# A mixture-of-experts block on one core: the last expert's down weights loaded early, and the sums at the end rearranged

## The reference, cut to what matters

```python
h = rmsnorm(x, norm_ffn_w)
logits = h @ w_router + b_router
top_logits, top_idx = lax.top_k(logits, 4)              # 4 of 32 experts
top_w = softmax(top_logits)
# for each expert e, over the tokens that chose it:
gu = xb @ w_gate_up[e] + b_gate_up[e]                   # 1024 -> 2048
gate = min(gu[:, ::2], 7.0); up = clip(gu[:, 1::2], -7.0, 7.0)
act = (up + 1.0) * (gate * sigmoid(gate * 1.702))
ys = act @ w_down[e] + b_down[e]                        # 1024 -> 1024
# y[token] = sum over its 4 choices of top_w * ys
out = rmsnorm(x + y, norm_final_w)
```

## Time and profile before

| | us |
|---|---|
| median of 3 runs | 1920.76 |
| lowest, highest | 1917.67, 1920.85 |
| the profiled execution | 1917.87 |
| its span, first to last instruction | 1916.1 |
| TensorE busy | 1861.3 |
| VectorE busy | 643.6 |
| ScalarE busy | 283.4 |
| GpSimd busy | 253.6 |
| mean granted TensorE clock | 0.99 of 2.4 GHz |

### The profile page before, as it was taken

The page is one execution under the profiler, slowest core; times in us unless marked ns, Lnnn a source line. Parts: engine busy times, 40 slices in busy tenths (PEclk is TensorE's granted clock), DMA queues, the critical chain, the costliest instruction groups (busy, mean ns, idle before and its releaser), DMA issues.

```text
span 1916.1 us, 40809 instructions
## 1 busy us (share of the span) xinstructions
PE 1861.3 (97%) x17222; PEld 870.7 (45%) x17222; DVE 643.6 (34%) x1225; ACT 283.4 (15%) x563; POOL 253.6 (13%) x297
## 2 busy tenths in 40 slices
PE   7999999999999999998999999999999999999995
PEld 4455555555555444442343444434343444444343
DVE  2563553635632110145132222323131322223236
ACT  3233423323233000021000000000000000000002
POOL 0010010000100000013222212121212222121200
PEclk9999999999999999998999999999999999999997
DMA  9211110111102321427999999999999999999995
GB/s 384 81 67 50 44 41 34 45 51 45 45 23 83 121 88 66 168 87 279 396 419 418 419 418 418 418 418 420 417 420 418 420 418 419 418 419 419 418 399 214
DMA packets 82218, 495.46 MB, mean 259 GB/s; under 512 B 15188, under 2 KB 15868, under 8 KB 28256
## 3 DMA queue, kind: packets, MB, share of 16 engines
q1 hardware_dynamic: 72656, 478.49, 61.7%
q0 software_dynamic: 9488, 15.94, 2.2%
HBM read 478.00 MB, written 24.53 MB: 262 GB/s over the span
## 4 chain that ended last, share of the span: by engine, by line
PE 50%; DMA 1%; DVE 1%; DVEq 0%; issue 0%; SPq 0%; ACT 0%; ACTq 0%
PE ps L1076 33%; PE ps L1091 17%; DMA arena<-expert_rows 1%; DVE oaT L1507 0%; DMA arena<-h_rows,gix 0%; DVE oaT L1504 0%; DVEq L2198 0%; DVE arena L1507 0%; DVEq L2149 0%; SPq L528 0%; DVEq L2141 0%; ACT arena L1495 0%; DVE arena L1504 0%; DVEq L2091 0%; DVEq L2103 0%
## 5 line engine op out<-in xcount | busy, mean ns | idle before, releaser
L1076 PE MATMUL ps<-arena 128*32 128x512 f32 x5952 | 647.4, 594 | 3.7 <-DVE arena L1504 3.7
L1076 PEld LDWEIGHTS ps<-arena 128*32 128x32 f32 x5952 | 202.6, 110 | 430.0 <-issue 425.2
L587 PE MATMUL ps<-hT,arena 128*128 128x512 f32 x768 | 349.4, 596 | 1.2 <-DVE arena L1507 0.9
L1091 PE MATMUL ps<-arena,hT 128*32 128x256 f32 x6144 | 339.0, 380 | 9.5 <-DMA arena<-in_w_dn 9.5
L1091 PEld LDWEIGHTS ps<-arena,hT 128*32 128x32 f32 x6144 | 209.0, 110 | 146.8 <-issue 29.5
L1504 DVE TENSOR_TENSOR arena<-ps,arena 128x768 f32<-128x768 f32 x64 | 58.3, 953 | 581.9 <-PE ps L1076 581.8
L587 PEld LDWEIGHTS ps<-hT,arena 128*128 128x128 f32 x768 | 138.4, 190 | 143.8 <-issue 139.6
L2259 POOL DMA_INDIRECT expert_rows<-hT,six x90 | 90.4, 1004 | 682.1 <-ACT hT L1158 663.7
L1451 ACT ACTIVATE arena<-arena 128x768 f32<-128x768 f32 x32 | 27.0, 844 | 696.5 <-DVE arena L2104 696.5
L587 PE MATMUL ps<-arena 128*128 128x512 f32 x256 | 120.2, 611 | 4.4 <-DVE arena L1504 2.2
L2247 POOL DMA_INDIRECT arena<-h_rows,gix x93 | 95.3, 1025 | 48.9 <-POOL gix L2244 27.2
(11 more groups left out here) (251 smaller groups left out, 1232.6 us busy)
## 6 DMA issues: line engine op xcount, KB each, us to landing
arena<-in_w_gu SPq DMA_DIRECT2D x256, 1024.0 KB, 16.4
arena<-in_w_dn SPq DMA_DIRECT2D x128, 1024.0 KB
arena<-in_w_pair SPq DMA_DIRECT2D x16, 1024.0 KB, 4.8
arena<-in_w_merge SPq DMA_DIRECT2D x16, 1024.0 KB, 4.8
expert_rows<-oaT SPq DMA_DIRECT2D x4, 2048.0 KB, 25.5
arena<-expert_rows SPq DMA_DIRECT2D x16, 512.0 KB, 15.1
arena<-in_x SPq DMA_DIRECT2D x8, 512.0 KB, 6.2
arena<-in_w_qb SPq DMA_DIRECT2D x4, 768.0 KB, 5.0
```

The lines of the kernel that those rows point to most:

```text
L587: ins = pe.matmul(region(name)[:, cols], lhsT, rhs, start=(k == 0), stop=(k == n - 1))
L1076: ins = pe.matmul(gu[32 * j:32 * (j + 1), g, :], columns[:, g, k, :], ring[k][:, 512 * j:512 * (j + 1)], start=(k == 0), stop=(k == KD - 1))
L1091: ins = pe.matmul(yd[32 * j:32 * (j + 1), g, 0:256], aT[:, g, 2 * c + k, :], ring[8 + c][:, D * k + 256 * j:D * k + 256 * (j + 1)], start= ...
```

## The change

The four down chunks of expert 31 no longer go through `ring[8..11]` at the end. They are loaded right after expert 0's own down chunks and the last tile of h2, into places of their own: parts of `hT`, `obT` and `oaT` that nobody uses later. For that, `tab`, `taby`, `tok` move together in `obT`, `wmT` and `bias_now` move to the arena, the running sum stays in `x2` in place of `acc`, and the last norm's weights go to `spare`.

VectorE transposes the last activations into a place of their own (`last_aT`, in the masks), so it doesn't wait for `down(30)`; it builds the join tables right after, the first and the second each with its own signal; then slots 0 to 2, then slot 3 by tile. All four tiles are finished by VectorE, each tile's finish behind the parts of the next. SP loads slots 0 to 3 one after the other, and the last norm's weights behind them. TensorE does tile 0's biases and first join, then `down(31)`, then the second join. The rows of extra blocks go to a second table `late_dram`, which is cleared like the first one, during pair 0 of the mixer.

```diff
@@ SP @@
+                if i == 0:
+                    for t in range(NT):
+                        sp.dma_start(late_dram[t * P * TOPK:(t + 1) * P * TOPK, :].rearrange("(p k) d -> p k d", k=TOPK),
+                                     zero_rows.unsqueeze(1).broadcast_to([P, TOPK, D])).then_inc(y_clear, 16)
...
             keep_rows(NT - 1)
+            def last_down_weights(c):
+                sp.dma_start(last_down[c], w_dn_chunk(NE - 1, 8 + c)).then_inc(last_down_in, 16)
+            last_down_weights(0)
+            ready(sp, f"lg{NT - 1}")
+            last_down_weights(1)
+            ready(sp, "x0_0", "x0_1")
+            sp.wait_ge(h2_st, 16 * NT)
+            last_down_weights(2)
+            last_down_weights(3)
             sp.wait_ge(table_set, 16 * NT * TOPK)
...
-            sp.dma_start(nrow, norm_final.broadcast_to([P, D])).then_inc(row_in, 16)
             sp.wait_ge(xT_done, NE - 1)
             sp.dma_start(tokens, token_row.broadcast_to([P, SEQ])).then_inc(row_in, 16)
-            for k in range(2):
-                early_slot(k)
-            down_weights(NE - 1, NE - 1)
-            for k in range(2, TOPK):
-                early_slot(k)
+            for k in range(TOPK):
                 sp.wait_ge(gu_used, 8 * (NE - 1) + 2 * k + 2)
                 sp.wait_ge(scattered, 16 * QUADS * min(NE - TOPK + 1 + k, JOINED[0]))
                 for t in range(NT):
+                    sp.dma_start(yin[k][:, t, :], slot_rows(y_dram, k, t)).then_inc(slot_in[k] if k < TOPK - 1 else rows_in[t], 16)
+            sp.dma_start(last_nrow, norm_final.broadcast_to([P, D])).then_inc(last_nrow_in, 16)
...
             for t in range(NT):
-                if t < AWAY:
-                    sp.wait_ge(all_rows, t + 2)
-                else:
-                    sp.wait_ge(out_done, t + 1 - AWAY)
+                sp.wait_ge(out_done, t + 1)
@@ TensorE @@
-            down(NE - 1)
...
             join(0, ys, 0)
+            last_expert_down()
+            pe.wait_ge(wm_done, 3)
             pe.wait_ge(ys_done, NE)
             join(1, last_ys, 0)
@@ ScalarE @@
-                if t < AWAY:
-                    ac.drain()
-                    copy(yin[1][:, t, :], acc[:, t, :], scale=r4[:, 1, t:t + 1]).then_inc(xn_done, 1)
...
-                if t:
-                    last_root(t - 1)
-            last_root(NT - 1)
+                last_root(t)
@@ VectorE @@
             activations(NE - 1)
-            activation_columns(NE - 1)
+            dv.transpose(last_aT.rearrange("p g b m -> p (g b m)"), act.rearrange("p g f -> p (g f)")).then_inc(aT_done, 1)
...
             for t in range(NT):
                 dv.wait_ge(rows_in[t], 48)
                 add_rows(TOPK - 1, t)
                 dv.drain()
-                add_parts(acc, t).then_inc(sum_done, 1)
+                if t:
+                    root(t - 1)
+                add_parts(t).then_inc(sum_done, 1)
                 dv.sem_inc(bo_kept, 1)
                 if t:
-                    root(t - 1)
-            for t in range(AWAY, NT - 1):
-                finish(t)
+                    finish(t - 1)
             root(NT - 1)
             finish(NT - 1)
@@ GpSimd @@
-            for t in range(AWAY):
-                po.wait_ge(xn_done, 2 * NT + t + 1)
-                po.tensor_tensor(x2[:, t, :], yin[1][:, t, :], nrow, ALU.mult).then_inc(all_rows, 1)
```

More of the change, by code:

```diff
@@ L537, in _ @@
             with sp.If(extra > 0):
-                sp.wait_ge(early_sums, TOPK - 1)
-                for t in range(NT):
-                    sp.wait_ge(rows_in[t], 48)
+                sp.wait_ge(bo_kept, NT)
                 with sp.Fori(0, MAX_EXTRA) as j:
@@ L1080, in up, with down_products, down @@
                         beside[k]()
-            def down(n):
+            def down_products(columns, weights, c):
+                for k in range(2):
+                    for g in range(QUADS):
+                        for j in range(4):
+                            ins = pe.matmul(yd[32 * j:32 * (j + 1), g, 0:256], columns[:, g, 2 * c + k, :],
+                                            weights[:, D * k + 256 * j:D * k + 256 * (j + 1)],
+                                            start=(c == 0 and k == 0), stop=(c == 3 and k == 1))
+                ins.then_inc(dn_used, 1)
+            def down(n, loads_before=0):
                 if not first(n):
@@ L1086, in down, with last_expert_down @@
                 for c in range(4):
[L1087 to L1094, removed]
+                    pe.wait_ge(chunk_in[8 + c], 16 * n + 16 - 16 * loads_before)
+                    down_products(aT, ring[8 + c], c)
+            def last_expert_down():
+                pe.wait_ge(last_down_in, 64)
+                pe.wait_ge(ys_done, NE - 1)
+                pe.wait_ge(aT_done, NE)
+                for c in range(4):
+                    down_products(last_aT, last_down[c], c)
             def expert(n):
@@ L1149, in _ @@
                         up(j + NE)
-                        down(j + NE)
+                        down(j + NE, loads_before=1)
         @block.scalar
@@ L2175, in _ @@
                 dv.wait_ge(again_in, 16 * NT * TOPK)
-                for k in range(TOPK - 1):
+                for k in range(TOPK):
                     add_slot(k)
+                dv.drain()
+                dv.memset(yin[TOPK - 1], 0.0)
                 for t in range(2):
@@ L2230, in _ @@
             po.wait_ge(tok_ready, 1)
-            po.wait_ge(y_clear, 16 * NT)
+            po.wait_ge(y_clear, 32 * NT)
             po.wait_ge(h2_st, 16 * NT)
@@ L2249, in gather, with scatter @@
                                           bounds_check=SEQ * 4 - 1, oob_is_err=False).then_inc(gathered, 16)
-            def scatter(n, q, passed=0):
+            def scatter(n, q, passed=0, into=y_dram):
                 if not first(n):
@@ L2258, in scatter @@
                 for g in range(QUADS):
-                    po.indirect_dma_start(out=y_dram.rearrange("r (j d) -> (r j) d", j=4),
+                    po.indirect_dma_start(out=into.rearrange("r (j d) -> (r j) d", j=4),
                                           out_offset=bass.IndirectOffsetOnAxis(ap=six[:, g:g + 1], axis=0),
@@ L2286, in _ @@
                         gather(j + NE, q)
-                        scatter(j + NE, q, passed=len(JOINED))
+                        scatter(j + NE, q, passed=len(JOINED), into=late_dram)
                         wait_past(scattered, 16 * QUADS * j + 16 * QUADS * (NE + 1 - len(JOINED)))
             po.sem_inc(all_rows, 1)
-            po.wait_ge(row_in, 48)
-            for t in range(AWAY):
-                po.wait_ge(xn_done, 2 * NT + t + 1)
-                po.tensor_tensor(x2[:, t, :], yin[1][:, t, :], nrow, ALU.mult).then_inc(all_rows, 1)
 def constants():
```

59 lines of the change are left out of this document (32 added, 27 removed).

## The result

The changed kernel took 1909.02 us in the median of five runs (1906.42 to 1909.33), the kernel before 1917.94 (1917.04 to 1920.85): and the ratio on record for the two sets of runs is 0.9946, 95% interval 0.9933 to 0.9959 (the two medians alone would give 0.9953). That is 0.5% faster, where 1909.5 was forecast. The profiled execution took 1906.42 us with a span of 1904.5, the lowest of the five; against the profiled execution of before it is 11.6 us shorter in the span, while the medians are 8.9 us apart.

What follows compares the result with a forecast made beforehand. TensorE bounds the loop, only just; bytes bound the end, 4 MB of weights then 4 MB of expert rows. -12.6 + 2.5 + 0.5 = -9.6 us gives 1908.3 or 1911.2, middle 1909.5; 8-in-10 range 1904.5 to 1915.

Steps and rivals of the forecast that it cites:

- The front: Four early loads before the table's read: they end near 884 to 885, delaying it 0.5 us, bounds 0 to 2.4.
- The start of slot 3: VectorE at the end: slot 3's first tile starts at 1881.6 instead of 1894.18, 12.6 us earlier.
- an end that was priced too high: From slot 3's first tile to the last store: 24.4 us, where before it was 21.9.
- the first rival: Before the loop, the table's completion waits for loads in flight: 1911.5, or 1912 with TensorE's clock; chance 0.14.
- The tile's step: VectorE at the end, per tile: slot 3, root, parts and finish in one row, 5.3 us.
- the rearrangement: VectorE's new order at the end, with two finishes back on VectorE: costs 2.5 us.
- The lead of about 3 us: Expert loop's weight stream: beyond 3 us of lead, pushed-in loads make TensorE wait at the last experts; 1916.5; chance 0.04.
- Slow landing of slots 2 and 3: At the end, rows come late: 1917 if slot 2 lands at 1884, 1913 more likely; chance 0.12.
- The blocked table: Before the loop, early loads ending after 885.9 hold up the table's read and TensorE; up to 1924; chance 0.04.
- The zeros: 8 MB more of writes for late_dram in the mixer's pair 0: cost taken as 0.
- TensorE's path: At the end: second join done at 1882.4, VectorE wants the parts at 1883.1; 0.7 us behind the bound, not showing.
- the signs that I had named: Table read within 1 us of 885.9, hole before up(1) 3.7 to 4.5 us, VectorE not waiting for rows, steps 5.3.

Runs made afterwards that it cites:

- late weights: The changed kernel with expert 31's four down chunks issued at the end again, between slots 1 and 2; 1921.06 us.
- the weights behind the table: The changed kernel with all four early chunks issued behind the table's read, in front of expert 1's chunks; 1916.61 us.
- two and two: The changed kernel with two early chunks loaded in the idle stretch, the other two behind the table's read; 1911.9 us.
- the quarter experiment: The changed kernel with only the last of the four early chunks loaded behind the table's read; 1908.24 us.
- the version with both away: The changed kernel with the last multiplication of tiles 0 and 1 on ScalarE and GpSimd again; 1907.2 us, then 1907.18.
- the control's profile: Profile of the changed kernel itself, run again unchanged beside other versions; median 1908.33 us, the profiled execution 1910.96.

## Why the prediction was right, step by step

The forecast of 1909.5 was met at 1909.02, and the cause was the right one: the bytes at the end were the bound, and with the loads at the end the gain is gone (1921.06). The terms were less exact than their sum, and that the sum came within 0.5 us is in part luck. It was counted from 1919.1, about the middle of two levels at which the three runs of before seemed to lie (the exact middle would have made it 1909.7); the median of five was then 1917.94, and the 28 runs of the first set fill the range from 1915.8 to 1921.2 without two levels. From 1917.94 the same -9.6 us give 1908.3. And a front and a start of slot 3 that were priced too low stand against an end that was priced too high.

**The front** was priced at 0.5 us of a possible 2.4, and here the first rival happened. Where no load is in flight at the last scatter, it completes in 3.64 us (before), 2.29, 2.64 and 2.23 (the kernels with late weights, with the weights behind the table, and with two and two); where the four early loads are, in 5.04, 5.33, 5.63, 5.01, 6.14, 6.22 and 4.59; with three loads in front, which are through near 883, in 3.06. The means are 2.7 and 5.4 us, so the loads cost such a scatter some 2.7 us, a little over the upper bound that I had from the gathers. The loads ended where I had them, near 885; what failed is the step from there, that a scatter which meets only their last microseconds loses 0.5 us. In the changed kernel it landed 2 us after they were through, about what an idle scatter takes in all. The rule that the Trainium skill states on the page "DMA: Bandwidth & Descriptors", section "Queues, rings and completion order", that a semaphore's increment lands only after every earlier write of its DMA engine, made this the likelier, and I gave it 0.14. The traces agree with it in direction; they don't tell it from a scatter that merely gets its turn late among large loads.

What this costs TensorE is less certain. From h2's store to the start of `down(0)` it is 56.7 to 57.8 us in the seven profiles with four loads in front (56.7 in the changed kernel), 54.2 with three, 53.7 with two and 52.3 with none (the kernel with late weights; 54.5 with the weights behind the table, where `up(1)` waited for its own weights). But the kernel before, with none either, took 56.5 us: there TensorE waited 3.72 us for `activations(0)` and ran the first part of `up(1)` at 1.2 GHz (granted clock 0.50 from 904 to 908), 23.70 us in all, while in the changed kernel the wait moved into `up(0)` (1.78 us in front of the extra list) and `up(1)` took 22.50. So against the changed kernel with fewer early loads the front costs 2.5 us or more, and between the two profiles of before and after it doesn't show: `down(30)` starts only 0.28 us later than before. How much of it the time of the runs holds stays open.

**The start of slot 3,** T, was forecast at 1881.6 and came at 1882.88. Slot 0 starts 0.56 us later than forecast: the join tables end at 1866.67, 0.2 us after the 1866.5 that I had (where my own terms, 1862.4, 1.0 and 2.79, add up to 1866.2), and 0.48 us of waiting for its rows come on top. The three slots take the 15.0 us that I had given them, with 0.40 us of waits for rows in it, and the last 0.69 us are a gap before slot 3's first tile, for which the sum had nothing. I had the rows of slots 2 and 3 landing 4 us ahead of their use, from the volume in flight. The quarter experiment shows that there is no such margin at slot 0: TensorE 1.9 us earlier gave 2.04 us of waiting for it.

**The tile's step** was the term most off. I summed 5.3 us, the finishes show 4.54: the 0.6 us between a tile's parts and the next instruction was read from the first tile of before, where it was 0.63; in the steps it is 0.28; the drain and the root between slot 3 and the parts take 0.50 instead of 0.80, and a finish runs into the next slot 3 without the gap of 0.1. The end took 21.6 us, not 24.4, so the rearrangement cost nothing against the 21.9 of before instead of 2.5. But its two finishes do cost 2.3 us, as the version with both away shows; in the kernel before they were saved and spent again on the collision (1.2 us) and on waits.

Together: -11.3 for T and -0.3 for the end make the 11.6 us between the two spans, where I had -9.6. The medians show 8.9 because the changed kernel's profiled execution was its fastest, while that of before lay at its median. The forecast gain of 9.6 us so lies between the two, 0.7 above the medians' and 2.0 below the profiles'.

**The rivals.** The lead of about 3 us was right in size: 10 us pushed in made the loop 6.3 us longer, 5 us 2.8, and 2.5 us 0.5, which is 2 to 3.7 us swallowed each time. What I missed is that the stream doesn't end with the weights: the rows stand behind them. Slow landing of slots 2 and 3 didn't come; all waits for rows in the changed kernel add up to 0.9 us, and to 1.8 in the control's profile. The blocked table was priced rightly as a whole (1915.9 for loads that end 6 us or more past the table's scatter), with its hole in `up(0)`. The zeros cost nothing, as said. TensorE's path was to be 0.7 us behind the bound: its second join ends at 1883.15, VectorE takes the parts at 1884.41, so it is 1.3. Of the signs that I had named, three failed: the table was read 1.25 us after 885.9, not within one; the hole before `up(1)` was 2.25 us, not 3.7 to 4.5, for part of it lay in `up(0)`; and VectorE did wait for rows, if only for 0.9 us.

## What to carry to other kernels

Where the end of a kernel waits for bytes, look in the table by windows for a stretch in which the DMA engines idle and SBUF has places that nobody uses any more, and load the last weights there; ask first which small transfer in that stretch lies on a chain of waits, for here the loads in flight made one take 2.7 us longer. Read the time to landing along a loop, not in one place: its growth tells how much lead the stream has and how much can be pushed into it. And let the work of an idle engine stay where it is if it starts after the busy one: handing two multiplications to the bound engine cost 2.3 us here by the profiles, 1.2 to 1.8 by the medians.

## What the hardware showed that I had not expected

A scatter of a few hundred bytes took 2.2 to 3.6 us to complete with the DMA engines idle, 4.6 to 6.2 when the last of 4 MB of loads were still in flight, and 7.1 where the loads had just been issued; a read of the 72 KB pieces of the table behind them reached VectorE after 7.7 instead of 3.3 us.

A stretch of TensorE at a lower clock cost little here where a wait followed. In the changed kernel the granted clock between 896 and 900 was 0.57 of 2.4 GHz after a wait of 1.78 us at 895, and 24 matmuls there took 4.48 us instead of 2.78; with three loads in front there was no such wait, and they took 2.78. But the wait before `up(1)` was 2.25 us in the first and 3.20 in the second, and from the table's read to `up(1)` it was 18.6 and 18.3 us. Where the slow stretch falls into `up(1)` itself, as before the change, that takes 23.70 instead of 22.50 us, and from the table's read to `down(0)` it is 41.8 instead of 40.9 us.
